# Attention weights of a three-stage transformer kernel: softmax factors applied by the turning product instead of by separate scalings

## The reference

```python
# first block, per branch; gblk holds the sigmoid gates of the three branches
p_w = masked_softmax(s_w, mask_w)
o_w = jnp.einsum('bghqk,bgkd->bghqd', p_w.astype(v_wb.dtype), v_wb)
return gblk[..., 0:1] * o_c + gblk[..., 1:2] * o_s + gblk[..., 2:3] * o_w
# second block
s = jnp.where((kpos[None, :] <= qpos[:, None])[None, None], s, -jnp.inf)
p = jax.nn.softmax(s, axis=-1).astype(v.dtype)
return jnp.einsum('bhqk,bkhd->bqhd', p, v)
# odd layer, differential heads
c = rms_norm(o[:, :, :C_HEADS] - lam * o[:, :, C_HEADS:], subln) * (1.0 - lam_init)
```

## Time and profile before

| | before |
|---|---|
| median of 3 runs | 1337.02 us (1333.85 to 1341.55) |
| profiled execution | 1336.98 us, its span 1335.2 us |

### The profile page before, as it was taken

The page is one execution under the profiler, slowest core; times in us unless marked ns, Lnnn a source line. Parts: engine busy times, 40 slices in busy tenths (PEclk is TensorE's granted clock), DMA queues, the critical chain, the costliest instruction groups (busy, mean ns, idle before and its releaser), DMA issues.

```text
span 1335.2 us, 26996 instructions
## 1 busy us (share of the span) xinstructions
PE 1273.4 (95%) x10439; PEld 1207.9 (90%) x10439; DVE 837.0 (63%) x1344; ACT 613.1 (46%) x887; POOL 539.4 (40%) x565
## 2 busy tenths in 40 slices
PE   7999999999999999999999889999999998879977
PEld 7999999999999998999999668999999997679856
DVE  5775558786555566555556785755556676856577
ACT  5444335344334455444335675533444346544373
POOL 4555444326444434444442243544443000820034
PEclk8999999999999999999999889999999999999998
DMA  8787754666776637666645214666654445234401
GB/s 261 227 238 216 216 173 143 189 189 198 227 228 194 191 123 212 181 196 195 189 148 177 63 39 131 180 194 195 195 174 135 144 150 198 83 114 139 153 25 60
DMA packets 275264, 223.11 MB, mean 167 GB/s; under 512 B 8114, under 2 KB 256454, under 8 KB 275068
## 3 DMA queue, kind: packets, MB, share of 16 engines
q1 hardware_dynamic: 272672, 216.11, 52.9%
q0 software_dynamic: 1504, 4.49, 1.7%
q10 hardware_dynamic: 1020, 1.58, 0.4%
HBM read 216.93 MB, written 4.19 MB: 166 GB/s over the span
## 4 chain that ended last, share of the span: by engine, by line
PE 81%; DVE 10%; ACT 4%; issue 2%; POOL 2%; DMA 1%; DVEq 0%; SPq 0%; ACTq 0%; POOLq 0%
PE psum L745 24%; PE psum L747 23%; PE psum L746 23%; DVE hn_tiles L1748 2%; POOL arena L2379 1%; DVE wal L1730 1%; PE psum L936 1%; ACT hn_tiles L1334 1%; DMA raw_a<-in_attn_w_q 1%; PE psum L938 1%; PE psum L937 1%; PE psum L702 1%; DVE hres L1796 1%; DVE wal L1943 1%; ACT pbuf L1520 1%
## 5 line engine op out<-in xcount | busy, mean ns | idle before, releaser
L745 PE MATMUL psum<-hn_tiles,wah 128*128 128x256 f32 x1976 | 553.8, 280 | 10.5 <-issue 4.2
L2392 POOL TENSOR_TENSOR wbl<-raw_b,wbh 128x256 fp32r<-128x256 f32 x412 | 401.6, 1005 | 397.0 <-ACT wbh L1262 380.1
L746 PE MATMUL psum<-hn_tiles,wah 128*128 128x256 f32 x1976 | 547.6, 277 | 0.0
L747 PE MATMUL psum<-hn_tiles,wal 128*128 128x256 f32 x1976 | 547.4, 277 | 0.0
L745 PEld LDWEIGHTS psum<-hn_tiles,wah 128*128 128x128 f32 x1976 | 370.8, 188 | 16.6 <-issue 12.0
L746 PEld LDWEIGHTS psum<-hn_tiles,wah 128*128 128x128 f32 x1976 | 370.6, 188 | 1.6 <-issue 1.4
L747 PEld LDWEIGHTS psum<-hn_tiles,wal 128*128 128x128 f32 x1976 | 370.7, 188 | 0.0
L1730 DVE TENSOR_TENSOR wal<-raw_a,wah 128x2048 fp32r<-128x2048 f32 (+3 forms) x127 | 292.8, 2306 | 108.0 <-ACT wah L1255 107.1
L1255 ACT ACTIVATE wah<-raw_a 128x2048 fp32r<-128x2048 f32 (+2 forms) x125 | 235.5, 1884 | 77.8 <-PE psum L747 49.4
L1380 ACT ACTIVATE gate_hid<-tmp 128x256 f32<-128x256 f32 x88 | 36.7, 417 | 411.9 <-DVE tmp L1860 411.9
L745 PE MATMUL psum<-hidh,wbh 128*128 128x256 f32 x768 | 212.6, 277 | 0.9 <-DVE hidl L1784 0.9
(11 more groups left out here) (321 smaller groups left out, 1626.7 us busy)
## 6 DMA issues: line engine op xcount, KB each, us to landing
raw_a<-in_ffn_w_in SPq DMA_DIRECT2D x176, 512.0 KB, 5.0
raw_b<-in_ffn_w_out SPq DMA_DIRECT2D x88, 512.0 KB, 4.3
raw_a<-in_w_in_even SPq DMA_DIRECT2D x15, 1024.0 KB, 5.1
raw_a<-in_conv_w_in SPq DMA_DIRECT2D x24, 512.0 KB, 4.3
raw_a<-in_w_in_odd SPq DMA_DIRECT2D x11, 1024.0 KB, 5.1
raw_a<-in_w_kv SPq DMA_DIRECT2D x6, 1024.0 KB, 6.1
raw_b<-in_conv_w_out SPq DMA_DIRECT2D x8, 512.0 KB, 5.7
raw_a<-in_attn_w_q SPq DMA_DIRECT2D x4, 1024.0 KB, 6.8
```

The source lines that it names most:

```text
L745: mm(dst, wh, xh, start=start, stop=False)
L746: mm(dst, wh, xl, start=False, stop=False)
L747: return mm(dst, wl, xh, start=False, stop=stop)
L2392: x = g.tensor_tensor(low[:, c], full[:, c], high[:, c].bitcast(F32), ALU.subtract)
```

## The change

The product with the identity that turns the exponents becomes a product with diagonal matrices that hold the factors. For a full duo, DVE writes four diagonals of 128 x 128 (two heads, two query halves) in one operation into `gate_hid`, two buffers in turn, and PE multiplies each block of 128 x 128 exponents (stationary) by its diagonal (moving) as an ordinary fp32 product. For a differential duo the two maps are turned and added in PSUM, six products instead of three transposes. POOL no longer takes part in `attend`, and DVE no longer scales full duos; small duos stay as they were. `p0_scaled` and `p1_scaled` become one semaphore, `scale_ready`, and DVE waits for the products of duo g - 2 before it writes the diagonals of g. As `gate_hid` is now in use during attention, `ukv` is loaded after the even attention and behind the rows of `w_out_even`, and the gain row moves to `arena`.

```diff
+        def diagonal(g):
+
+            return gate_hid[:, g % 2 * 2:g % 2 * 2 + 2, :].rearrange("p m (t c) -> p m t c", t=2)
...
-        gain_row = gate_hid[:, :, :].rearrange("p a c -> p (a c)")
+        gain_row = arena[:, 16:20].rearrange("p a c -> p (a c)")
...
+        DUOS = {"nsa": 24, "even": 4, "odd": 8}
...
+            load_rows(a["w_out_even_2"][0], OUT_ORDER["even"])
+            sp.wait_ge(S("pt_ready"), DUOS["nsa"] + DUOS["even"])
             sp.dma_start(ukv, a["mla_w_ukv_2"][0]).then_inc(S("latent_w_loaded"), 16)
-            load_rows(a["w_out_even_2"][0], OUT_ORDER["even"])
...
-                        pe.wait_ge(S("p0_scaled"), g + 1)
-                        if du["kind"] == "full" and du["coef"] != "lambda":
-                            pe.wait_ge(S("p1_scaled"), fulls(name, j))
+                        pe.wait_ge(S("scale_ready"), g + 1)
                         if g >= 1:
                             pe.wait_ge(S("pt_copied"), g)
                         merged = du["coef"] == "lambda"
                         for i in range(1 if merged else 2):
                             p, b = probs(g)[:, i], bank[6 + i]
                             if du["kind"] == "full":
-                                pe.transpose(b[:, 0:P], p[:, T:384], ident)
-                                pe.transpose(b[:, P:T], p[:, 0:P], ident)
-                                x = pe.transpose(b[:, T:384], p[:, P:T], ident)
+                                for at, lo, t in ((0, T, 0), (P, 0, 1), (T, P, 1)):
+                                    for m in (0, 1) if merged else (i,):
+                                        x = mm(b[:, at:at + P], probs(g)[:, m, lo:lo + P], diagonal(g)[:, m, t, :],
+                                               start=m == 0 or not merged, stop=m == 1 or not merged)
...
-                        if du["coef"] == "lambda":
-                            cuts = ((0, T, 1), (T, 384, 0))
-                            for lo, hi, i in cuts:
-                                x = v.tensor_scalar(p[:, 0, lo:hi], p[:, 0, lo:hi], rs[:, s0, i:i + 1], None, ALU.mult)
-                            link(x)
-                            for lo, hi, i in cuts:
-                                x = v.scalar_tensor_tensor(p[:, 0, lo:hi], p[:, 1, lo:hi], rs[:, s0 + 1, i:i + 1],
-                                                           p[:, 0, lo:hi], ALU.mult, ALU.add)
-                        elif du["kind"] == "full":
-                            x = v.tensor_tensor(p[:, :, T:384], p[:, :, T:384], rs[:, r, 0:1].to_broadcast([P, 2, P]),
-                                                ALU.mult)
+                        if du["kind"] == "full":
+                            if g >= 2:
+                                v.wait_ge(S("pt_ready"), g - 1)
+                            x = v.tensor_tensor(diagonal(g), ident[:, None, None, :].to_broadcast([P, 2, 2, P]),
+                                                rs[:, r, :, None].to_broadcast([P, 2, 2, P]), ALU.mult)
                         else:
                             p = p[:, :, 0:2 * NC].rearrange("p m (i n) -> p m i n", i=2)
                             x = v.tensor_tensor(p, p, rs[:, r, :, None].to_broadcast([P, 2, 2, NC]), ALU.mult)
-                        x.then_inc(S("p0_scaled"), 1)
+                        x.then_inc(S("scale_ready"), 1)
...
-            def attend(name):
-                for st, du in enumerate(STAGES[name]):
-                    g_ = DBASE[name] + st
-                    g.wait_ge(S("rs_ready"), g_ + 1)
-                    if du["kind"] == "cmp" or du["coef"] == "lambda":
-                        continue
-                    for i in range(2):
-                        r, p = 2 * (g_ % ND) + i, probs(g_)[:, i, 0:T]
-                        x = g.tensor_scalar(p, p, rs[:, r, 1:2], None, ALU.mult)
-                    x.then_inc(S("p1_scaled"), 1)
-
             def mix(name):
-                attend(name)
```

More of the change, by code:

```diff
@@ L666, in build @@
         STAGES = {"nsa": nsa_duos(), "even": even_duos(), "odd": odd_duos()}
[L667 to L668 removed]
+        DBASE, UBASE = {}, {}
+        m0 = u0 = 0
         for name, duos in STAGES.items():
[L670 removed]
+            DBASE[name], UBASE[name] = m0, u0
             m0 += len(duos)
[L672 removed]
             u0 += duos[-1]["unit"] + 1
[L675 to L677 removed]
         TILE_COUNT = {"nsa": {c: c + 1 for c in range(8)}, "even": {0: 9, 1: 10, 2: 11, 3: 12, 4: 13, 5: 13, 6: 14, 7: 14},
```

6 lines of the change are left out of this document (removed).

## The result

The changed kernel takes 1346.97 us (median of 6 runs, 1344.19 to 1349.62), the kernel before in the same runs 1336.74 us (1333.85 to 1341.72). The ratio is 1.0075 with the interval 1.0055 to 1.0096: slower by 10.2 us, on the upper side of the predicted range and 5 us above the predicted time. The profiled execution took 1346.85 us (span 1345.1).

The account below looks back on a forecast made before the run. PE was taken as the bound (81% of the chain). 1337.0 + 2.6 (first stage) - 0.3 (second) + 2.7 (third) = 1342.0 us, own range 1338 to 1346, 8-in-10 range 1334 to 1349.

Parts of the forecast that it names:

- rival 1: Whole kernel: products replace transposes, PE idles less, the clock holds up better; together -6.4 us, to 1335.6; chance 0.19.
- signs of being wrong: First-stage period not 8.1 us, a second slow stretch there, or VectorE waiting over 0.5 us before its diagonals.
- PE's new price: Attention stages: 0.111 us a pass, +0.67 us per full duo, +1.0 per lambda duo; 20.1 us of PE work.
- Rival 3: PE's products cost over 0.111 us a pass: 1367 us with exposed loads, 1379 at four times; chance 0.03.
- The waits: First stage: PE's 4.75 us of idle waits shrink to 0.5 without GpSimd's step, -4.3 us.
- GpSimd's 48 scalings leave the chain: Attention stages: scalings of 2.05 us a duo leave the path; from factors to PE's start takes 0.7 us instead.
- rival 4: First stage: ScalarE's copies, not GpSimd, release PE; waits give 2.5 us less, 1344.5 us; chance within the forecast's 0.58.
- The clock: First stage: the second half-clock stretch goes, 9.6 us at 0.43 each, -4.1 us; the first, 6.0 us, stays.
- rival 2: First stage: VectorE becomes the bound if its new wait costs 0.5 us a period or more; 1348 us; chance 0.18.
- The second stage: VectorE sets the end: diagonals +0.27 or +0.9 us, GpSimd's earlier lows about -1; net -0.3 (-1.5 to +1.5).
- The third stage: +6.7 us of PE work at 3.3 us a step, partly absorbed by idle time; net +2.7 us (1.8 to 3.5).
- PE's idle time absorbs some 4: Third stage: PE's 8.9 us of idle time, including the wait before the first set, takes up some 4 us.

Follow-up runs that it names:

- the unscaled kernel: The kernel before with the scalings of full and differential duos left out on both engines, transposes kept; 1334.31 us, ratio 0.9979.
- half diagonals: The changed kernel with VectorE writing one diagonal a head, from one query half's factors, used for both halves; 1347.51 us, ratio 1.0064.

## Why the prediction was right, and where not

**In the wide range, but not in the forecast's own.** The time, 1347.0 us, lies inside 1334 to 1349, but outside the 1338 to 1346 that the forecast gave itself with 0.58, and outside of "within 0.5%", in the "slower" that had 0.36. That it landed in the wide range is partly luck: two terms of the sum failed, by mechanism and not only by size. The first stage cost +7.7 for +2.6, the second -0.8 for -0.3, the third +4.3 for +2.7; the tail gave back 1.0 us that only rival 1 had named. Of the signs of being wrong one showed, VectorE's wait for PE before its diagonals (1.0 us for 0.5); the other two, a clean period other than 8.1 and a second slow stretch, did not.

**PE's new price: right in kind, 0.08 us a duo too low.** 0.119 us a pass in the first stage instead of 0.111 makes a full duo +0.75 for +0.67, 1.3 us over 16 duos. Two duos at +0.75 on a period of 6.76 would be 8.26; it is 8.05, because 6.76 was not quite free of pauses: the small duos' turning started 0.67 to 0.73 us after its scores in the kernel before (793.65 and 800.35), and 0.55 in the changed one. That the clean period met the predicted 8.1 is two small errors against each other. Rival 3 falls, and with it, for this use, the factor of four that the Trainium skill gives ("TensorE: Matmul & The Clock Gate", Terms): a block costs 2 x 0.119 us as a product and 0.11 us as a transpose, a factor of 2.2.

**The waits: the number came out, the reason did not.** PE's idle time fell by 4.0 us where 4.3 were predicted. But 2.4 of them fell in the first part, where the prediction took 0 and where the idle time varies between executions (0.95 us in the second of the kernel before, 2.2 in the second of the changed one). And the 4.75 us that the prediction started from were too many: the earlier trace rows show 0.23 us of idle PE before 770.04, not 1.1 (and so 1.8 of the 3.6 us before the second slow stretch, not 2.7), which leaves some 3.8. Above all, the unscaled kernel, without GpSimd's step and without VectorE's, has as much idle time as the kernel before (9.4 for 9.6 us; in the second part 7.3 for 6.4 and 6.2), while products beside all scalings bring the second part's from those 6.4 and 6.2 to 3.0. What fills PE's idle time is PE's own longer work. The step that failed is, for the first stage, "GpSimd's 48 scalings leave the chain": they left it, and the next one, ScalarE's copies behind VectorE's late tasks, was due at nearly the same moment. This is rival 4 in a stronger form than I gave it. I priced it at 2.5 us; it took the whole relief, but for the 1.3 us or so that GpSimd's early low halves may hide.

**The clock: -4.1 us that never came.** As predicted, no half-clock stretch stands near 770 us in the changed kernel. But the first, which was to stay at 6.0 us "because what PE did before it is unchanged", was 16.8 us long (the two stretches of the first profile, 6.0 and 9.6 us in the prediction, are 6.8 and 10.4 us from end to end). Half-clock time in the stage is 17.2 us before and 16.8 after. I took one execution's stretches for the kernel's own; the second execution of the kernel before has 13.6, 3.6 and 3.1 us where the first had 6.8 and 10.4, and one execution of the same first stage after has only 3.6. Here is the largest part of the miss: 4.1 us, and the products in the longer first stretch at double price.

**VectorE as the bound: rival 2 came, by another way.** I gave the new wait of VectorE for PE's products 0.5 us a period or more as its condition; the wait was 1.0 us in the whole stage, once (at 762.26). Yet VectorE bounds three periods, from the fifth pair's scores to the eighth's, with rounds of 8.9 us where I had computed 8.7 and trusted two steps of lead to hide four of them. The diagonals cost 2.9 us beside the same products without them, half of them give 1.6 back, and 1.3 us of it is GpSimd's early work beside VectorE (these three are not a sum). That last effect I had counted only where it helped, in the second stage.

**The second stage** gained 0.8 us (-0.3 predicted), and holding the lows back costs 0.6 of it: the reason holds, but it is a part only. Beside products, leaving the scalings out is worth 3.3 us there and the diagonals take 1.1 back (35.07 to 36.19), while the passes cost 1.4 (36.99 to 38.35) beside the scalings and 0.5 (34.56 to 35.07) without; the prediction gave PE slack there and priced only the last duo's +0.27. The second execution of the kernel before had 36.5 us, so the gain is 0.3 to 0.8. The transfer of `ukv` stayed covered, as predicted: nothing waits for it.

**The third stage** had the right work (PE busy +6.1 us for +6.7) and the right step of 3.3 us, without a gap from 1285.8 to 1302. What failed is "PE's idle time absorbs some 4": it fell by 1.8 us, from 8.9 to 7.1. The first wait was in the list of those that absorb; it grew from 3.22 to 3.46 through GpSimd's low halves.

**Open.** Why the clock fell a second time at 752 in most executions and not in one is not settled by these runs. In the six profiled executions with transposes the stage had 13.6 to 24.0 us at half clock (mean 18.9), in the eight with products 3.6 to 20.4 (mean 13.2). This leans the way of the Trainium skill's remark that transposes don't count as PE being busy in the same way ("TensorE: Matmul & The Clock Gate", Part 4), but the two sets overlap. The one pair that differs in nothing else, the kernel before and the same with products, has 17.2 and 20.3 us against 14.0, too few executions to tell.

## What to carry to other kernels

The engine that ends a wait need not own it: before a helper's step is bought off the path with work on the bounding engine, leave the step out altogether, and see, stage by stage, whether the bounding engine waits any less (in the first stage it did not, 7.3 us of its second part against 6.4 and 6.2; in the second stage, where VectorE ends the stage, leaving it out was worth 2.4 us). Work taken from one engine starts something else on it earlier; ask whose operations that will lie beside. And a half-clock stretch seen in one profile is one draw: don't book its removal as a gain before a second profile of the same kernel shows it at the same place.

## What the runs showed of the hardware that I had not expected

- VectorE operations with two SBUF inputs lose 0.28 to 0.50 us beside GpSimd's subtractions, and the loss hardly follows their size: 0.17 became 0.51 us for 4 elements a row, 0.22 became 0.50 and 0.72 for 60, 0.42 became 0.92 for 256 (with half diagonals, at 791.88), 0.69 became 1.18 for 512.
- With the same instructions in the same order PE was granted half speed for 3.6 to 16.8 us of the first stage, and the stage took 74.9 to 78.95 us. From the third pair on, at full clock, three executions agree to 0.02 us (60.18 to 60.20).
- A reciprocal of half the width takes more than half the time, 0.94 to 0.95 us for 1.75, and the multiplication behind it 0.35 to 0.51 for 0.48.
